# A hybrid encoder trunk on one core: the first unit's way from its last inverse level to the expert scores, in a new order

## What is computed

```python
h = rms_norm(x); p = h @ W_in
y_A = differential attention (4 heads, block-causal), softmax(p0) - lam * softmax(p1)
y_B = S5 state-space layer, gelu, gated by sigmoid(yg @ w_glu), rms_norm
y_C = RWKV-7: S = S * w_t + sa * b_t + v_t * k_t per step, from S0 = 0; y = S r_t
x = x + concat(y_A, y_B, y_C) @ W_out
q = rms_norm(x) @ w_q                      # 8 heads x 2 halves x 128
s = q . sub_keys; top 16 of each half; top 16 of the 256 sums -> 16 experts per head
x = x + sum over 128 experts of gate * gelu(u_row . h) * v_row
```

## Time and profile before

| | |
|---|---|
| median of 3 runs | 1729.08 us (1728.06 to 1729.99) |
| the profiled execution's own time | 1729.59 us |
| its span in the trace | 1727.8 us |
| busy share of the span | DVE 80%, PE 78%, POOL 66%, ACT 24% |
| gather DMA (queue q0) | 538.25 MB, 80.0% of 16 engines' span |
| weight and other DMA (queue q1) | 100.96 MB, 16.2% |

### The profile page before, as it was taken

The page is one execution under the profiler, slowest core; times in us unless marked ns, Lnnn a source line. Parts: engine busy times, 40 slices in busy tenths (PEclk is TensorE's granted clock), DMA queues, the critical chain, the costliest instruction groups (busy, mean ns, idle before and its releaser), DMA issues. The chain is left out here.

```text
span 1727.8 us, 17677 instructions
## 1 busy us (share of the span) xinstructions
PE 1339.9 (78%) x5322; PEld 755.4 (44%) x5322; DVE 1390.0 (80%) x3383; ACT 406.1 (24%) x977; POOL 1137.9 (66%) x1046
## 2 busy tenths in 40 slices
PE   6989689688889397867887868978888837765667
PEld 6568444255456163444454453444545412222222
DVE  7867999996779789996777898987777897687663
ACT  2442312333211221413221122313221121101000
POOL 2002776777775876477767777577777777777773
PEclk9999899999999699999999979989999969988889
DMA  7348999999999999899999999999999999999997
GB/s 236 135 158 284 398 403 362 410 382 365 408 402 399 404 393 405 313 357 355 385 393 404 403 404 407 366 375 354 387 403 402 409 410 409 410 409 410 409 409 313
DMA packets 204721, 640.89 MB, mean 371 GB/s; under 512 B 18602, under 2 KB 35860, under 8 KB 204628
## 3 DMA queue, kind: packets, MB, share of 16 engines
q0 software_dynamic: 147920, 538.25, 80.0%
q1 hardware_dynamic: 56172, 100.96, 16.2%
q10 hardware_dynamic: 536, 0.57, 0.1%
HBM read 638.65 MB, written 1.05 MB: 370 GB/s over the span
## 5 line engine op out<-in xcount | busy, mean ns | idle before, releaser
L618 POOL DMA_INDIRECT arena<-in_peer_u_dram,expert x512 | 562.0, 1098 | 346.1 <-issue 139.7
L618 POOL DMA_INDIRECT arena<-in_peer_v_dram,expert x512 | 566.3, 1106 | 210.2 <-issue 139.3
L2430 PE MATMUL bank<-arena,diag 128*128 128x512 f32 x768 | 433.8, 648 | 242.4 <-DMA arena<-in_peer_v_dram,expert 171.1
L1835 DVE SCALAR_TENSOR_TENSOR arena<-arena,normed 128x1024 f32<-128x1024 f32 x364 | 434.5, 1225 | 63.0 <-DMA arena<-in_peer_u_dram,expert 58.6
L2431 PE MATMUL bank<-arena,diag 128*128 128x512 f32 x768 | 416.9, 626 | 0.0
L2430 PEld LDWEIGHTS bank<-arena,diag 128*128 128x128 f32 x768 | 133.8, 199 | 453.7 <-issue 386.9
L2431 PEld LDWEIGHTS bank<-arena,diag 128*128 128x128 f32 x768 | 154.3, 201 | 200.3 <-issue 200.3
L1833 DVE SCALAR_TENSOR_TENSOR arena<-arena,bank 128x1024 f32<-128x1024 f32 x148 | 176.9, 1219 | 80.7 <-DMA arena<-in_peer_u_dram,expert 80.1
L1057 ACT ACTIVATE diag<-ident,weight 128x128 f32<-128x128 f32 x384 | 129.9, 392 | 211.5 <-DVE weight L1852 119.6
L1910 PE MATMUL bank<-h_cm,wring 128*128 128x128 f32 x1152 | 143.6, 287 | 27.8 <-DMA wring<-in_peer_w_q_dram 8.4
L1910 PEld LDWEIGHTS bank<-h_cm,wring 128*128 128x128 f32 x1152 | 141.3, 202 | 39.6 <-issue 24.5
(11 more groups left out here) (445 smaller groups left out, 1534.7 us busy)
## 6 DMA issues: line engine op xcount, KB each, us to landing
wring<-in_w_in_dram SPq DMA_DIRECT2D x40, 1024.0 KB, 12.9
wring<-in_peer_w_q_dram SPq DMA_DIRECT2D x25, 1024.0 KB, 15.0
wring<-in_w_out_dram SPq DMA_DIRECT2D x16, 1024.0 KB, 8.9
arena<-in_peer_u_dram,expert POOLq DMA_INDIRECT x512, 12.8
arena<-in_peer_v_dram,expert POOLq DMA_INDIRECT x512, 13.7
arena<-in_peer_w_q_dram SPq DMA_DIRECT2D x7, 1024.0 KB, 11.5
wring<-in_w_in_dram SPq DMA_DIRECT2D x4, 512.0 KB, 13.2
x<-in_x_dram SPq DMA_DIRECT2D x2, 512.0 KB, 5.3
```

The lines of the kernel that those rows point to most:

```text
L618: nc.gpsimd.indirect_dma_start(out=rows[g % RING], out_offset=None, in_=tables[kind], in_offset=bass.IndirectOffsetOnAxis(ap=expert[:, n % ...
L1835: ins = stt(row, row, 1.0, hb, ALU.mult, ALU.mult, accum_out=dots[:, slot:slot + 1])
L2430: mm(bank[6][:, :], d, row[:, 0:512], start=first, stop=end)
```

## The change

All of it lies in unit 0, but for the products with the carried state, which also go in unit 2 (the first tile of layer 1).

- No products with a zero state: where t is 0, L2146 and L2163 go, and on DVE the memset and scaling of the state (`own(V.memset(...))` and two tensor_scalar at L1387).
- `outputs_begun`: the two products per head that need no solution of the inverse are taken out of `outputs` and put on PE ahead of the last `level_update`, into free parts of bank 7; DVE copies them out and later adds the rest.
- PE's order: the last level's product ahead of the turned probabilities; `solve` ahead of `o_length`; out0 ahead of `s5_glu`; `s5_sum` behind out1.
- ACT: one-element activations that only make the table load stand earlier, ahead of the Square (Sqrt), behind the attention root (Gelu), behind the Tanh (Sqrt).
- DVE: `outputs` ahead of `s5_gated`.
- The expert part: the first query chunk is multiplied in pieces (columns 0-1, 2-3, 4-7 of the eight blocks) between the transposes, with only the first group of keys turned ahead of its end; the other three groups come behind the first scores.
- Loads: q0 and keys change places in the ring; the early chunks q1 to q7 move up by two row buffers (q7 now in 14 and 15), and another selection of them (q1, q5, q6, q7) is loaded ahead of out2.

```diff
-EARLY = {(0, f"q{i}"): 2 * i - 2 for i in range(1, PEER_HEADS)}
+EARLY = {(0, f"q{i}"): 2 * i for i in range(1, PEER_HEADS)}
@@ PLAN
+    if _n == 0:
+        PLAN += [(_n, "q0"), (_n, "keys")] + [(_n, name) for name in Q_NAMES[1:]]
+        continue
@@ SP
-                    for early in ("q1", "q2", "q6", "q7"):
+                    for early in ("q1", "q5", "q6"):
                         load(0, early)
+                    sp.wait_ge(qkT_ps, 2)
+                    load(0, "q7")
@@ ACT first()
                     values()
+                    product(6)
                     turned_probs(0)
-                    product(6)
+                    turned_probs(1)
                     updated(6)
-                    turned_probs(1)
+                    own(A_(small_a[:, 30:31], eps[:, 0:1], ACT.Sqrt))
                     o_squares()
+                    solved()
                     o_roots()
-                    solved()
+                    own(A_(small_a[:, 30:31], eps[:, 0:1], ACT.Gelu))
                     s5_gelu()
                     s5_tanh()
+                    own(A_(small_a[:, 30:31], eps[:, 0:1], ACT.Sqrt))
                     s5_root()
@@ ACT peer()
-                if t == 0:
+                if t == 0 and n:
                     key_columns(0)
                     key_columns(1)
                 act.wait_ge(x_mid, n + 1)
...
-                if t == 0:
+                if n == 0:
+                    key_columns(0)
+                elif t == 0:
                     key_columns(2)
                     key_columns(3)
@@ DVE products() and first()
-                    if t == 0:
-                        own(V.memset(state[:], 0.0))
-                    for b in range(2):
-                        ins = ts(state0[:, b, :], state[:, b, :], small_m[:, 6 + b:7 + b], None, ALU.mult)
-                    own.add(ins)
+                    if t:
+                        for b in range(2):
+                            ins = ts(state0[:, b, :], state[:, b, :], small_m[:, 6 + b:7 + b], None, ALU.mult)
+                        own.add(ins)
...
                     s5_back_im()
+                    outputs_begun()
                     o_scale()
                     attended()
                     s5_skip()
+                    outputs()
                     s5_gated()
-                    outputs()
@@ PE
+                def outputs_begun():
+                    pe.wait_ge(all_masked, 1)
+                    pe.wait_ge(tok_ok, 1)
+                    pe.wait_ge(z_ok, 2)
+                    for i, par, pr, ps_ in heads:
+                        mm(early_y[ps_, pr, :], tok[:, 0, pr, ps_], rkT[:, i, :], start=True, stop=True)
+                        last = mm(early_state[ps_, pr, :], tok[:, 2, pr, ps_], tok[:, 0, pr, ps_], start=True, stop=True)
+                    last.then_inc(early_ps, 1)
@@ PE first()
                     right_side()
+                    level_product(6)
                     pe.wait_ge(v_ok, 1)
                     turn_probs(0)
                     turn_probs(1)
-                    level_product(6)
+                    outputs_begun()
                     level_update(6)
                     attend()
+                    solve()
                     o_length()
-                    solve()
                     pe.wait_ge(z_ok, 2)
                     s5_output()
                     outputs()
-                    s5_glu()
                     pe.wait_ge(mix_d, 1)
                     to_model(0, "out0")
-                    s5_sum()
+                    s5_glu()
                     means()
                     to_model(0, "out1")
+                    s5_sum()
                     variances()
@@ PE peer()
                 turn_half(0)
-                if t == 0:
+                if n == 0:
+                    pe.wait_ge(fT_a, 1)
+                    first_query((0, 1))
+                elif t == 0:
                     turn_keys(0)
                     turn_keys(1)
                 yield "fT"
                 turn_half(1)
-                if t == 0:
+                if n == 0:
+                    first_query((2, 3))
+                    turn_keys(0)
+                    pe.wait_ge(fT_v, 1)
+                    first_query((4, 5, 6, 7))
+                elif t == 0:
                     pe.wait_ge(x_mid, n + 1)
```

More of the change, by code:

```diff
@@ L545, in _ @@
                     sp.wait_ge(st_b, 1)
-                    sp.wait_ge(st_cps, 1)
                     sp.wait_ge(st_bps, 1)
-                    for early in ("q1", "q2", "q6", "q7"):
+                    for early in ("q1", "q5", "q6"):
                         load(0, early)
+                    sp.wait_ge(qkT_ps, 2)
+                    load(0, "q7")
                 if (n, name) == (1, "bc0"):
                     sp.wait_ge(mix_s, 1)
-                    for early in ("q3", "q4", "q5"):
+                    for early in ("q2", "q3", "q4"):
                         load(0, early)
@@ L1031, in peer @@
                     if n == 0 and g == 0:
+                        for i in (1, 2, 3):
+                            key_columns(i)
                         normed_copied(0)
@@ L1528, in right_side @@
                     dve.wait_ge(rhs_ok, n + 1)
+                def outputs_begun():
+                    dve.wait_ge(early_ps, 1)
+                    V.tensor_copy(rw["y"][:, :, :], early_y)
+                    own(V.tensor_copy(state[:, :, :], early_state))
                 def outputs():
@@ L2145, in right_side @@
                         dst = rhs_half(n, par)[:, HD * pr:HD * pr + HD]
-                        mm(dst, rw["al"][ps_, pr, :], state0[ps_, pr, :], start=True, stop=False)
-                        last = mm(dst, nT[:, i, :], tok[:, 0, pr, ps_], start=False, stop=True)
+                        if t:
+                            mm(dst, rw["al"][ps_, pr, :], state0[ps_, pr, :], start=True, stop=False)
+                        last = mm(dst, nT[:, i, :], tok[:, 0, pr, ps_], start=t == 0, stop=True)
                     last.then_inc(rhs_ps, 1)
@@ L2357, in turn_keys @@
                     for b in range(4):
-                        last = tr(quad((0, 1, 4, 5)[i])[:, b, :], keys[:, 4 * i + b, :], ident[:, :])
+                        last = tr(quad(key_bank(n, i))[:, b, :], keys[:, 4 * i + b, :], ident[:, :])
                     if i < 3:
@@ L2369, in turn_half, with first_query @@
                     last.then_inc(fT_ps, 1)
+                def first_query(ks):
+                    w = chunk(0, "q0").rearrange("p (k c) -> p k c", c=256)
+                    for j in range(2):
+                        for k in ks:
+                            last = mm(bank[6 + j][:, 0:P], w[:, k, P * j:P * j + P], hb_cm[:, k, :], start=k == 0, stop=k == KD - 1)
+                    if ks[-1] == KD - 1:
+                        last.then_inc(chunk_done, 1)
                 yield "fsc"
                 turn_half(0)
-                if t == 0:
+                if n == 0:
+                    pe.wait_ge(fT_a, 1)
+                    first_query((0, 1))
+                elif t == 0:
                     turn_keys(0)
@@ L2388, in key_scores @@
                         pe.wait_ge(key_ok, 4 * layer + 4)
+                    elif n == 0 and g == 0:
+                        pe.wait_ge(key_ok, 1)
                     if g >= (2 if n else 4):
@@ L2398, in peer @@
                     g = TOP_OF[hd]
-                    if hd == 0:
+                    if hd == 0 and n:
                         pe.wait_ge(fT_a, n + 1)
@@ L2403, in peer @@
                             pe.wait_ge(key_ok, 4 * layer + 2)
+                    if n == 0 and hd == 0:
+                        key_scores(0)
+                        pe.wait_ge(x_mid, 1)
+                        for i in (1, 2, 3):
+                            if i == 3:
+                                pe.wait_ge(key_ok, 1)
+                            turn_keys(i)
+                        continue
                     if n:
@@ L2410, in peer @@
                             pe.wait_ge(pq_ok, NT * n + g - 1)
+                            pe.wait_ge(key_ok, 4)
                         to_columns(n, name, g % 2, hd - TOP[g][0])
```

41 lines of the change are left out of this document (29 added, 12 removed).

## The result

The changed kernel takes 1726.11 us, median of 22 runs (1721.44 to 1731.06); the kernel before, on the same chip, 1730.38 (22 runs, 1726.30 to 1735.32). The ratio is 0.9973, 95% interval 0.9964 to 0.9982: 4.7 us faster, 3.1 to 6.2 (the two medians alone lie 4.3 apart). Forecast were 7.1 us and 1722.0; the time lies above the range. The profiled execution took 1728.18, its span is 1726.4.

A forecast was written before the change was run, and what follows sets the result against it. The chain up to DVE's first choosing operation starts the gather, which follows rigidly with DVE and DMA full; its steps bring that start from 149.45 to 142.3, 7.1 us earlier: 1722.0 against the median 1729.08, range 1719.5 to 1725.5.

The forecast's parts named there:

- Steps 1 to 6: Unit 0 from right_side to the attention's reciprocal: reciprocal begins at 111.25 instead of 115.53, 4.3 us earlier.
- Rival C: ACT stands still behind a table load for 1.28 us, ahead of the Square: only 5.8 us earlier, 1723.3; 2%.
- Step 7: PE takes out0 before s5_glu, 115.45 to 119.0; s5_gated on DVE at 121.0 instead of 124.31, 3.3 us earlier.
- Rival E: PE's lower clock moves into out0, out1 and out3, 3.6 us more each; all three give 1733, 3.7 slower; 4%.
- rival B: Part lost to lower clock at the length, late keys, or right_side and early products: 3.6 to 6.0 us left; 20%.
- Steps 8 and 9: From out1 to the first query: out3 at 130.8 instead of 136.97; DVE's first choosing operation at 142.3, 7.1 us earlier.
- Rival D: The shift is real but used up later in the gather: under 3.5 us remains, 1725.6 to 1729; 8%.
- a gather longer by more than 2 us: Sign of being wrong: the gather's stretch longer than before by more than 2 us; forecast was the same within 1 us.
- no clock fall at 109 to 116: Expected in the profile after: PE's clock does not drop in that time, around the length, forecast at 109.3 to 110.4.

The follow-up runs named there:

- e1_warm: Changed kernel plus eleven unused identity products on PE in the idle time ahead of out0; median 1724.08 us, right_side to first gather 51.76 instead of 53.52.
- e6_tables_late: e1_warm without the three one-element activations, so each table load stands where it did before; right_side to first gather 1.38 us longer than in e1_warm.
- e4_delay20: Changed kernel plus six reciprocals on DVE (20.3 us) ahead of the first choosing operation; 15.2 us above the kernel before.

## Why the prediction was wrong

**Steps 1 to 6 held**, within 0.4. With the 0.96 added: the level product 101.48 (forecast 101.5), the update 105.0 (105.4, since the early products took 1.2 and not 1.7), the Square 108.4 (108.65), the length 109.06 at 1.13 (109.3 at 1.1), the reciprocal 111.07 (111.25). The table load ahead of the Square costs what the row said: 105.92 plus 1.28, the one-element activation at 107.22, the Square at 107.45. Rival C did not come about: the trace has 0.02 us between the load's end and the next activation. The Trainium skill's page "ScalarE: Activation LUTs", section "What ACT_TABLE_LOAD costs", adds a drain of 1380 ns, which this trace doesn't have.

**Step 7 failed**, in the words "out0 first, 115.45 to 119.0 (eight products, 3.70 with the tail". Out0 began at 115.26, as said, and took 5.40, because PE had idled for 2.83 us ahead of it and its clock fell (e1_warm). Everything behind it is late by about this: s5_gated 122.5 (121.0), s5_normed 126.9 (125.3), out3 132.4 (130.8), first choosing operation 143.95 (142.3). That is 1.65 late there after 0.2 early at the reciprocal: 1.85 for 1.70 to 1.80 of out0. Rival E had named this mechanism, but only as three outputs hit at once or two that undo the gain; rival B had the lower clock at the length, which it left, not at the place to which it went. One output chunk at the lower clock, half of it, stood nowhere. (The description of the kernel and step 7 count eight products in a chunk; the program has four, each listed twice, and the times are not touched by this.) The argument against E, that gaps of 1.09 had not lowered the clock, was from gaps less than half as long as the one that the new order opens, which rival E itself had put at 2. It was right for out2, where PE waited 1.79 and the clock stayed at 1.00. e1_warm shows what the idle time ahead of out0 cost, 1.76 us. The Trainium skill's page "TensorE: Matmul & The Clock Gate", section "Why this matters for your kernels", advises against idle gaps between bursts of products; e1_warm agrees, while the 3.07 ahead of out2 in e6_tables_late cost no clock.

**Steps 8 and 9 held as distances**: from out0's end to the first choosing operation 23.3 were forecast, measured 23.3 in both e1_warm (117.97 to 141.27) and the changed kernel (119.70 to 142.99). PE turned the keys at 138.70, 139.7 on the forecast's scale (138.1), and did not wait for them.

**Where the rest of the miss came from.** The time was 4.1 above the forecast (1726.11 against 1722.0). The base was 1.3 too low: 1729.08 from 3 runs, 1730.38 from 22. The stretch was 1.6 too long, by out0. The remaining 1.2 is inside the interval of the ratio (1.6 to either side), and no run resolves it: the shift in the profiles, 5.5, lies inside 3.1 to 6.2, the forecast's 7.1 outside it. The 5.5 in turn hangs on the first profile of the kernel before; with the mean of its two it is 6.3, just outside. A single execution scatters by 5 us to either side, most of it in the gather (1543 to 1552 in twelve profiles). Rival D, that the gather uses up more than half of the shift, names a range in which the time happens to lie (1725.6 to 1729), but no run speaks for its mechanism: e4_delay20 moved the end by 19.9 for 20.3, and the changed kernel's gather took 1549.0 in one profile and 1543.3 in the other. A smaller loss there is open. The three profiles in the old order have 1544.1 to 1545.4, the nine in the new order 1543.1 to 1552.2, on average 2.3 more, with a scatter too wide to call it a difference. Of the prediction's own signs of being wrong one came up, a gather longer by more than 2 us (1573.2 from first gather to the end of the span instead of 1568.2); the second profile (1567.2) shows that this sign was too fine for a single execution. Of what it said the profile would show, "no clock fall at 109 to 116" failed. My range had no room for an error of the base.

**What stays open.** Unit 2's part (eight products and three DVE operations less) was counted as nothing and is below what the runs resolve. Why the lower clock begins at different places in executions of the kernel before, and not in the changed one, is not settled: three profiles of the latter order agree (with e4_delay20), which may be chance. Nor is it settled why 2.83 us of idle time ahead of out0 lowered the clock and 3.07 ahead of out2 did not.

## What to carry over

When a new order brings PE's work forward and leaves it idle ahead of a long group of products, price that group at both clock levels, unless the trace shows a gap as long, behind work as dense, that did no harm. The length of the gap alone doesn't tell (2.83 lowered the clock, 3.07 did not). Filling the gap with products that nobody reads cost nothing here, since PE would have waited anyway, and gave 1.8 us. Fetching a table early paid where ACT had to wait meanwhile and the load would otherwise have stood on the chain: of three, one paid. For a change of a few microseconds in a program whose executions scatter by five, measure a stretch between two landmarks in each profile; the medians only confirm it.

## What the runs showed that I had not expected

- The lower clock moves rather than leaves: before it lay on attend, the length and `solve` (0.50 at 110 to 116), in the second profile also on the level product (0.50 at 104 to 106), with only the state's products gone on `s5_glu` and the start of out0 (0.59 at 118 to 122), after the change on out0 (0.50 at 116 to 118), and with `s5_glu` first on both (2.08 and 5.73). Only with the idle time filled was it absent from 98 to 136.
- Eight small products, four of 128 columns and four of 64, take 1.2 us (102.85 to 104.05); four of 64 columns alone take 1.00 in the earlier trace rows, and I had taken 1.7 for the eight.
- An idle time of 3.07 us ahead of out2, behind two output chunks at full clock, left the clock at 1.00 (e6_tables_late).
- The indirect gather of 1024 row sets takes 1543 to 1552 us in twelve executions, 1543.3 and 1549.0 in two of the same kernel.
